# Two row sums of a MoE layer's closing normalisation on GpSimd instead of VectorE, one turn of rows a product later, and 24 unread TensorE products

## What is computed

```python
x = layer_norm(DEEPNORM_ALPHA * x + mix, ln1_g[i], ln1_b[i])
moe = hier_moe(x, ...)                     # y = sum of two experts' outputs, each times its weight
x = layer_norm(DEEPNORM_ALPHA * x + moe, ln2_g[i], ln2_b[i])
gate = sigmoid(x @ ple_w_gate[i] + ple_b_gate[i])
x = x + gate * (p[i] @ ple_w_proj[i])
```

## Time and profile before

| | |
|---|---|
| median of 3 runs | 1281.59 us (1281.4 to 1281.94) |
| the profiled execution | 1281.04 us, span 1279.5 us |
| TensorE matmul busy | 1227.1 us, 96% |
| VectorE busy | 834.9 us, 65% |
| ScalarE busy | 558.0 us, 44% |
| GpSimd busy | 164.0 us, 13% |
| mean granted clock of TensorE | 0.983 |

### The profile page before, as it was taken

How to read it: one execution, slowest core, us unless ns; L and a number is a source line. 1 busy time by engine, 2 the same in 40 slices (tenths; PEclk the granted TensorE clock), 3 DMA queues, 4 the chain that set the end, 5 groups by cost and what they waited for, 6 DMA issues and landing times.

```text
span 1279.5 us, 19633 instructions
## 1 busy us (share of the span) xinstructions
PE 1227.1 (96%) x7659; PEld 1115.6 (87%) x7659; DVE 834.9 (65%) x1118; ACT 558.0 (44%) x627; POOL 164.0 (13%) x193
## 2 busy tenths in 40 slices
PE   7999999999999999899999799999999899999798
PEld 6888899999999998788878599999998788877598
DVE  4554477464474737789889785445434778989783
ACT  4322232213131222378787564112121368878651
POOL 2200010010000002013231001000002012232100
PEclk9999999999999999799999899999999899999899
DMA  9444254243242322469998553322312359999512
GB/s 337 153 158 156 104 158 144 93 150 119 78 152 73 126 77 101 161 259 378 374 377 302 195 168 101 99 67 93 105 69 85 141 198 366 388 396 346 211 50 75
DMA packets 85616, 229.76 MB, mean 180 GB/s; under 512 B 9798, under 2 KB 42702, under 8 KB 73136
## 3 DMA queue, kind: packets, MB, share of 16 engines
q1 hardware_dynamic: 66880, 179.84, 38.9%
q0 software_dynamic: 18672, 49.04, 10.8%
HBM read 210.15 MB, written 35.46 MB: 192 GB/s over the span
## 4 chain that ended last, share of the span: by engine, by line
PE 71%; DVE 13%; DMA 10%; ACT 3%; issue 2%; POOL 1%; DVEq 0%; SPq 0%; POOLq 0%; ACTq 0%
PE ps L1739 14%; PE ps L1741 14%; PE ps L1740 14%; DMA w_raw<-in_moe_w_gate_up 7%; PE ps L1790 3%; PE ps L1792 3%; PE ps L1791 3%; DVE w_lo L1169 3%; PE ps L2077 2%; PE ps L2079 2%; PE ps L2078 2%; ACT w_hi L853 2%; PE ps L1850 2%; DVE x_tok L1568 2%; PE ps L2041 1%
## 5 line engine op out<-in xcount | busy, mean ns | idle before, releaser
L1169 DVE TENSOR_TENSOR w_lo<-w_raw,w_hi 128x2048 fp32r<-128x2048 f32 (+1 forms) x133 | 290.5, 2191 | 70.4 <-ACT w_hi L853 69.6
L1739 PE MATMUL ps<-x_hi,w_hi 128*128 128x288 f32 (+2 forms) x1024 | 306.4, 299 | 8.8 <-DVE x_lo L1613 7.1
L1741 PE MATMUL ps<-x_hi,w_lo 128*128 128x288 f32 (+2 forms) x1024 | 303.9, 297 | 0.0
L1740 PE MATMUL ps<-x_lo,w_hi 128*128 128x288 f32 (+2 forms) x1024 | 303.9, 297 | 0.0
L853 ACT ACTIVATE w_hi<-w_raw 128x2048 fp32r<-128x2048 f32 (+1 forms) x133 | 242.7, 1834 | 79.3 <-PE ps L1741 61.6
L1739 PEld LDWEIGHTS ps<-x_hi,w_hi 128*128 128x128 f32 x1024 | 195.0, 190 | 9.9 <-issue 7.5
L1740 PEld LDWEIGHTS ps<-x_lo,w_hi 128*128 128x128 f32 x1024 | 194.9, 190 | 0.1
L1741 PEld LDWEIGHTS ps<-x_hi,w_lo 128*128 128x128 f32 x1024 | 194.8, 190 | 0.0
L1739 PE MATMUL ps<-g_hi,w_hi 128*128 128x288 f32 x384 | 114.8, 299 | 3.4 <-DVE g_full L1715 2.7
L1741 PE MATMUL ps<-g_hi,w_lo 128*128 128x288 f32 x384 | 113.9, 296 | 0.0
L1740 PE MATMUL ps<-g_lo,w_hi 128*128 128x288 f32 x384 | 113.7, 296 | 0.0
(11 more groups left out here) (295 smaller groups left out, 2123.3 us busy)
## 6 DMA issues: line engine op xcount, KB each, us to landing
w_raw<-in_moe_w_gate_up SPq DMA_DIRECT2D x34, 1024.0 KB, 11.0
w_raw<-in_moe_w_down SPq DMA_DIRECT2D x32, 1024.0 KB, 13.8
w_raw_more<-in_moe_w_gate_up SPq DMA_DIRECT2D x30, 1024.0 KB, 14.3
w_raw<-in_a_w_in SPq DMA_DIRECT2D x23, 1024.0 KB, 5.2
w_raw<-in_a_w_out SPq DMA_DIRECT2D x12, 1024.0 KB, 5.1
w_raw<-in_b_w_in SPq DMA_DIRECT2D x12, 1024.0 KB, 5.2
w_raw<-in_ple_w_gate SPq DMA_DIRECT2D x8, 1024.0 KB, 11.9
v_scratch<-v_stage POOLq DMA_DIRECT2D x6, 1024.0 KB, 4.5
```

What stands on the lines that cost most here:

```text
L1169: dve.tensor_tensor(unit_of(wlo, d), raw_unit(d), unit_of(whi, d).bitcast(f32), ALU.subtract).then_inc(split_done, 1)
L1739: pe.matmul(out, sh, mh, start=first, stop=False)
L1740: pe.matmul(out, sh, ml, start=False, stop=False)
L1741: ins = pe.matmul(out, sl, mh, start=False, stop=final)
```

## The change

For tiles 3 and 4, GpSimd multiplies the rows of k = 0 by their weights (in place) and adds them to `xtok`, instead of VectorE's `add_rows(i, 0)`; VectorE waits for that on a new semaphore before `add_rows(i, 1)`. Tile 2's two sums stand ahead of `lo(U_G[l] + 1)`. Tile 2 is turned after the gate product q = 2 and not q = 1. And TensorE makes 6, 6 and 12 products of a tile of ones, with 512 columns each, around the turns of tiles 0 and 1; they are written into the PSUM bank of q = 0 ahead of it, and nobody reads them. The wait for `atl_ok` moves ahead of them.

```diff
--- before.py
+++ after.py
@@ -358,6 +358,7 @@
         ov = [{n: sem(f"ovf_{n}{l}") for n in ("chain", "onehot", "idx", "idxcopied", "a", "stored", "product", "evicted")} for l in range(DEPTH)]
 
         w_ok, side_st, wsl_ok, ohw_ok = sem("weights_ready"), sem("zeros_stored"), sem("slot_weights"), sem("last_onehot_ready")
+        first_sum = sem("x2_first_summed")
         y_half, ol_done = sem("last_y_half_copied"), sem("last_rows_summed")
         n2_act = sem("x2_scaled_act")
 
@@ -833,6 +834,11 @@
                 pool.wait_ge(side_st, 32 * (l + 1))
                 expert_rows(NE - 2)
                 expert_rows(NE - 1)
+                for i in range(3, NT):
+                    t = tok(i)
+                    pool.wait_ge(yg_ld[i], 16 * (l + 1))
+                    ch.link(pool.tensor_scalar(yrows(i, t, 0), yrows(i, t, 0), wtop[0:t, 0, i:i + 1], None, ALU.mult))
+                    pool.tensor_tensor(xtok[0:t, i, :], xtok[0:t, i, :], yrows(i, t, 0), ALU.add).then_inc(first_sum, 1)
 
                 if l == 0:
                     pool.wait_ge(pe_ok, GQ)
@@ -1637,16 +1643,16 @@
                 scale2(0)
                 scale2(1)
                 first_part_low()
-                lo(U_G[l] + 1)
                 add_rows(2, 0)
                 add_rows(2, 1)
+                lo(U_G[l] + 1)
                 rstd2(2)
-                add_rows(3, 0)
+                dve.wait_ge(first_sum, (NT - 3) * l + 1)
                 add_rows(3, 1)
                 lo(U_G[l] + 2)
                 rstd2(3)
                 scale2(2)
-                add_rows(4, 0)
+                dve.wait_ge(first_sum, (NT - 3) * l + 2)
                 add_rows(4, 1)
                 tile_low(2)
                 scale2(3)
@@ -2227,13 +2233,21 @@
                         ins = pe.transpose(out_bank(u)[0:t, k * P:k * P + P], xk(xT, 4 * h + k, P * i, t), ident[:, :])
                     ins.then_inc(out_t, 1)
 
+                def keep_running(n):
+                    for _ in range(n):
+                        pe.matmul(ps[:, 0, :].rearrange("p (a t) -> p a t", t=P), ones_r[:, :],
+                                  ones_r[:, :].unsqueeze(1).to_broadcast([P, 4, P]), start=True, stop=True)
+
+                pe.wait_ge(atl_ok, NE * (l + 1))
+                keep_running(6)
                 n2_turn_rows(0)
+                keep_running(6)
                 n2_turn_rows(1)
-                pe.wait_ge(atl_ok, NE * (l + 1))
+                keep_running(12)
                 for q in range(GQ):
                     gate(q)
-                    if q in (1, 4, 6):
-                        n2_turn_rows((1, 4, 6).index(q) + 2)
+                    if q in (2, 4, 6):
+                        n2_turn_rows((2, 4, 6).index(q) + 2)
                     if l:
                         if q == 9:
                             pe.wait_ge(pe_ok, GQ + KT)
```

## The result

| | before | after |
|---|---|---|
| median, 5 runs each, in turns on one chip | 1281.59 us (1281.4 to 1282.72) | 1286.82 us (1286.04 to 1289.38) |
| ratio | | 1.0044, 95% interval 1.0033 to 1.0054 |
| the profiled execution, its span | 1281.04, 1279.5 us | 1286.82, 1285.2 us |
| GpSimd busy | 164.0 us | 189.3 us |
| q = 6, first product, layer 0 | 747.13 us | 749.38 us |

The change makes the kernel slower by 0.44%, some 5 us; the forecast was 1292.5 us, 11 us slower. In the changed kernel the lines of VectorE and TensorE stand six higher (L1613 is now L1619, L1602 (`x_low`) L1608, L1568 L1574, L1169 L1175, L1739 L1745, L2197 L2203), those of the row loads one higher (L631 is L632).

What follows compares the result with a forecast made beforehand. The prediction took VectorE's path to the last split before q = 6 as the bound. Its steps, with GpSimd and VectorE alternating at SBUF, cost 5.6 us a layer, 11.2 in all: 1292.5 us, range 1279.5 to 1298.

Steps and rivals of the forecast that it cites:

- The bound: The start of q = 6 on TensorE waits for VectorE's last split, `lo(U_G[l] + 3)`, at 747.09 us in layer 0.
- Products of ones, turn one product later: no term: Around TensorE's first turns and tile 2's turn: neither changes the time, since VectorE sets the start of q = 6.
- the cover that the text named: TensorE's slack ahead of q = 6: VectorE's path sets it; were that over 3 us shorter, the ones' effects would count.
- The rival with the ones: The products of ones become the bound because TensorE's clock falls anyway: no effect on time; no chance of its own given.
- Tile 2's sums ahead of the split: up to 1.6: VectorE, idle 1.64 us for ScalarE's root, splits in that time: up to 1.6 us gained on the path.
- Two sums spared: 2.4: VectorE is spared two instructions of 1.2 us on the path by GpSimd's sums: a gain of 2.4 us.
- The multiply and the add at 2.7 us each: GpSimd's instructions per tile: multiply 2.7 us from a row of 5.39 us for 128x2048; the add, without a row, taken alike.
- What the engines do to each other: GpSimd and VectorE take turns at SBUF; either holds access to its instruction's end, so GpSimd's 2.7 us delay VectorE.
- The wait for tile 4's pair, some 4 us: VectorE waits from about 742.5 to 746.6 us for GpSimd's 5.4 us multiply and add on tile 4, in each layer.
- VectorE is not held up: Rival, chance 0.17: GpSimd loses SBUF access to VectorE but never takes it away; 1280.8 us, no change.
- Faster: Rival, chance 0.13: VectorE not held up and GpSimd needs about 1 us per instruction; 2.8 us a layer gained, 1276 us.
- The sum: q = 6 in layer 0 at 752.7 instead of 747.09 us: 5.6 us a layer, 11.2 us for both.

Runs made afterwards that it cites:

- h_split_first_no_ones: The change without GpSimd's part and without the products of ones, with `lo(U_G[l] + 3)` ahead of `scale2(3)`: 1277.58 us, 0.9969 of the kernel before.
- c_ones_only: The kernel before, with only the products of ones (6, 6 and 12) around the first two turns added: 1282.99 us, 1.0007 of the kernel before.
- e_no_ones: The change without its products of ones, the `atl_ok` wait back behind the first two turns: 1287.67 us, 1.0053 of the kernel before.
- i_turn_as_before: The change without GpSimd's part, with tile 2 turned after q = 1 again: 1277.33 us, 0.9966 of the kernel before.
- a_no_pool: The change without GpSimd's part, both sums of tiles 3 and 4 back on VectorE: 1277.78 us, 0.9972 of the kernel before.
- the bench: VectorE and GpSimd alone, not the kernel's work: GpSimd multiplies and adds, first alone, then beside trains of VectorE instructions; multiply 2.85 us, add 2.34 us alone.
- b_pool_only: The kernel before with only GpSimd's first sums of tiles 3 and 4, orders as before, no products of ones: 1291.58 us, 1.0075 of the kernel before.

## Why the prediction was right, and where it was too high

**The bound** was right: q = 6 waits for the last split, in the changed kernel and in every other version but h_split_first_no_ones.

**Products of ones, turn one product later: no term.** Right for both, shown by c_ones_only, e_no_ones and i_turn_as_before. Even without the cover that the text named, the ones were worth nothing (h_split_first_no_ones), which it had not said: behind the cover lay another. The rival with the ones had rightly no effect. What the text did not have is the clock behind the new wait: the 3.24 us of idle in layer 1 were followed by half clock, which cost 2.4 us. It had said that the clock decides nothing; that was so of 722 to 726 us, which it named, and not of 1238 to 1243.

**Tile 2's sums ahead of the split: up to 1.6.** Measured 1.64 in the changed kernel's sum and 1.7 in a_no_pool.

**Two sums spared: 2.4.** Measured 2.63. The pairs are 2.60 us, and half of that is 1.3, not the 1.2 of the text.

**The multiply and the add at 2.7 us each.** The multiply alone is 2.85 in the bench (3.08 the first time); the add, which had no row before, 2.34 there and 2.40 in the kernel. The estimate of 2.25 us from the Trainium skill, "GPSIMD Engine Reference", section "Elementwise — side-by-side cycle accounting", was nearer than the 2.7 taken.

**What the engines do to each other** is the step that failed in size. "Whoever holds the access keeps it to the end of its instruction" was carried over from a row of the other direction. That GpSimd waits for a running VectorE instruction was seen again (the add's 2.83 us). In the other direction it holds for the add: 2.0 of its 2.4 us. It does not hold for the multiply, which keeps VectorE 0.78 us. And the place was wrong: GpSimd was put in front of each low part, 2.7 + 2.7 us; the text named as a sign against itself that the first low part follows the cast at once while GpSimd's multiply is running. The profile shows the low part following at once, but the multiply was issued 0.66 us after it had started, since the rows landed at 723.1 and not just after 722. The second low part did start under the running multiply, and wasn't longer. A multiply issued during the cast does hold the first one, as b_pool_only shows, but by 0.79 us and not by 2.7. From 5.4 us of hold to 2.79 is 2.6 us a layer, nearly all of the 3.1 by which cast to q = 6 was too high (30.7 by the text, 27.59); 0.2 more are the sums spared.

**The wait for tile 4's pair, some 4 us**: 3.96 and 3.95 measured, the best-placed term. The prediction had GpSimd's end 5.4 us behind the norm's; it is 5.2 behind it. Rows and norm both follow from the end of the same split, so the wait came out right although that split ended 3 us earlier than foreseen.

**The rivals.** "VectorE is not held up" (0.17) falls by the split of 4.29. But it was wrong at another place too: it took no account of a hold in which VectorE loses less than GpSimd's instruction lasts, the case that came. "Faster" (0.13) asked for a pair under 2 us; the pair is 5.2.

**The sum**: 2 x 5.6 = 11.2 foreseen. Measured 2.5 a layer in the stretch, less 1.6 regained between the layers, plus 2.4 of clock behind it. The last two were not foreseen and nearly cancel, which is luck: both hang on whether the clock fell behind a wait that could go either way. That 1286.8 lies in the stated range is in part luck too. The range's lower part stood for an add near 0.98 us, or for no hold at all. The add is 2.34 to 2.40; by the text's own sum that takes 0.3 us off two places in each layer and gives some 1291 us. Most of the rest of the way down is the hold, which the range had no case for between all and nothing.

Left open: why a multiply holds VectorE for 0.8 us and no longer, and at which instruction's start it gets in; and what decides whether TensorE's clock falls in a wait of 2.6 to 3.2 us. The reordered sums were not run with nothing else changed; that the gain is theirs follows from a_no_pool with c_ones_only and i_turn_as_before.

## What to carry to other kernels

Moving VectorE work to an idle GpSimd is no relief while VectorE works on SBUF: here two sums of 1.3 us a layer were spared and 2.8 to 5.5 us of hold taken for them, because GpSimd's add keeps VectorE's SBUF instructions out for nearly its own length. Give GpSimd work where VectorE waits or reads PSUM, and look at whose turn comes next; and count the whole helper's latency from the moment its data can be there, not only its length. And look at what a new wait does to TensorE's clock behind it: in the change's layer 1 that came to 2.4 us. The gain in this change was in the order: putting a ready split of 2.3 us into a wait of 1.64 us on the chain, once in each layer, gave 3.6 us, with no engine added.

## What was unexpected of the hardware

- The hold isn't symmetric, nor the same for all instructions: a GpSimd add of 128x1024 (2.34 us) costs a VectorE instruction 1.9 to 2.1 us, a multiply by a column (2.85 us) 0.7 to 0.85 us, and twice that beside instructions of 0.7 to 0.8 us; a multiply of 64x1024 0.61 to 0.65, an add of 64x1024 1.88.
- A multiply issued while VectorE runs back-to-back SBUF instructions waits for the running one; beside those of 1.2 us and more it let a second one pass in four of six cases of the bench (issued at 18.45, in at 20.54 us) and got in at once in two. Every add got in at the next start.
- VectorE instructions with one full-size SBUF source (copy, norm) are held as well; those that read PSUM are not, and don't hold GpSimd.
- With the unread products TensorE's clock reads 1.00 and not 0.72 over 722 to 732 us in the kernel otherwise as before, and they gave no time.
- Of eleven waits of TensorE of 2.57 to 3.24 us at the full clock, six were followed by half clock. Twins went different ways: 2.77 us in the change's two layers (0.52, then 1.00), 3.23 and 3.24 us in e_no_ones's.
